# Two broadcasts on the way to TensorE: tiled products of 64 stationary columns in place of widened copies and full turns

## What is computed

```python
qb = apply_rope_2(rms_norm(heads(gq, GQA_Q_HEADS), q_gain[l]), cos, sin)     # 8 query heads of 64
kb = apply_rope_2(rms_norm(heads(gk, GQA_KV_HEADS), k_gain[l]), cos, sin)    # 2 key heads of 64
...
def softmax_attn(q, k, v):
    s = jnp.einsum('bgrqd,bgkd->bgrqk', q, k).astype(jnp.float32) * SCALE
    p = jax.nn.softmax(s, axis=-1).astype(v.dtype)
    return jnp.einsum('bgrqk,bgkd->bgrqd', p, v)
```

## Time and profile before

| what | value |
|---|---|
| median of 3 runs | 1810.4 us (1808.3 to 1814.79) |
| span of the profiled execution | 1814.2 us; the longest of the three runs, 1814.79 us, is 0.6 us above it |
| mean granted clock of TensorE | 0.995 |
| busy: PE, PEld | 1765.5 us (97%), 1444.1 us (80%) |
| busy: DVE, ACT, POOL | 930.4 us (51%), 899.4 us (50%), 1346.3 us (74%) |
| chain that ended last | PE 88%, DVE 6%, ACT 3% |

### The profile page before, as it was taken

How to read it: one execution, slowest core, us unless ns; L and a number is a source line. 1 busy time by engine, 2 the same in 40 slices (tenths; PEclk the granted TensorE clock), 3 DMA queues, 4 the chain that set the end, 5 groups by cost and what they waited for, 6 DMA issues and landing times.

```text
span 1814.2 us, 29552 instructions
## 1 busy us (share of the span) xinstructions
PE 1765.5 (97%) x10046; PEld 1444.1 (80%) x10046; DVE 930.4 (51%) x1898; ACT 899.4 (50%) x1404; POOL 1346.3 (74%) x776
## 2 busy tenths in 40 slices
PE   9988999979999999999999999999999999999997
PEld 7767888867888897788888977788888977788886
DVE  4567665563554554455555564545456665441112
ACT  6455444566444555644445455554446445554343
POOL 7368998434988687588888874588886894678884
PEclk9999999999999999999999999999999999999999
DMA  7767786424887644357886462368774563346552
GB/s 273 193 205 243 240 270 212 143 88 156 286 264 241 212 147 156 127 181 223 261 257 225 154 185 86 113 206 269 253 248 159 170 208 99 117 151 196 186 186 69
DMA packets 268425, 347.27 MB, mean 191 GB/s; under 512 B 20264, under 2 KB 181416, under 8 KB 268328
## 3 DMA queue, kind: packets, MB, share of 16 engines
q1 hardware_dynamic: 265152, 339.40, 58.6%
q10 hardware_dynamic: 3176, 6.62, 1.2%
HBM read 342.20 MB, written 1.64 MB: 190 GB/s over the span
## 4 chain that ended last, share of the span: by engine, by line
PE 88%; DVE 6%; ACT 3%; issue 1%; DMA 1%; POOL 0%; SPq 0%; ACTq 0%; DVEq 0%; POOLq 0%
PE bank L2447 23%; PE bank L2449 23%; PE bank L2448 23%; PE bank L2586 3%; PE bank L3187 2%; PE bank L2515 1%; PE bank L2517 1%; PE bank L2516 1%; PE bank L3177 1%; PE bank L3226 1%; PE bank L2610 1%; PE bank L2570 0%; DVE X L1547 0%; ACT wh L844 0%; ACT xf L928 0%
## 5 line engine op out<-in xcount | busy, mean ns | idle before, releaser
L807 POOL TENSOR_TENSOR wl<-raw,wh 128x1024 fp32r<-128x1024 f32 x300 | 730.7, 2445 | 112.1 <-ACT wh L1009 86.9
L2447 PE MATMUL bank<-wh,xh 128*128 128x512 f32 (+1 forms) x1590 | 625.2, 393 | 9.2 <-POOL wl L795 2.5
L2449 PE MATMUL bank<-wl,xh 128*128 128x512 f32 (+1 forms) x1590 | 612.4, 385 | 0.0
L2448 PE MATMUL bank<-wh,xl 128*128 128x512 f32 (+1 forms) x1590 | 611.2, 384 | 0.0
L794 POOL TENSOR_TENSOR wl<-raw,wh 128x512 fp32r<-128x512 f32 (+1 forms) x232 | 310.0, 1336 | 323.1 <-ACT wh L844 312.6
L1009 ACT ACTIVATE wh<-raw 128x1024 fp32r<-128x1024 f32 x270 | 286.5, 1062 | 434.9 <-PE bank L2449 424.7
L2447 PEld LDWEIGHTS bank<-wh,xh 128*128 128x128 f32 x1590 | 299.6, 188 | 71.7 <-issue 5.6
L844 ACT ACTIVATE wh<-raw 128x1024 fp32r<-128x1024 f32 (+2 forms) x268 | 275.0, 1049 | 155.7 <-PE bank L2449 88.3
L2449 PEld LDWEIGHTS bank<-wl,xh 128*128 128x128 f32 x1590 | 299.3, 188 | 61.0
L2448 PEld LDWEIGHTS bank<-wh,xl 128*128 128x128 f32 x1590 | 300.0, 189 | 55.2
L795 POOL TENSOR_TENSOR wl<-raw,wh 128x512 fp32r<-128x512 f32 (+1 forms) x232 | 309.9, 1336 | 0.0
(11 more groups left out here) (414 smaller groups left out, 2030.0 us busy)
## 6 DMA issues: line engine op xcount, KB each, us to landing
raw<-in_w_ffn_in SPq DMA_DIRECT2D x264, 256.0 KB, 3.0
raw<-in_w_in SPq DMA_DIRECT2D x224, 256.0 KB, 3.0
arena<-in_w_mod SPq DMA_DIRECT2D x76, 512.0 KB, 5.2
raw<-in_w_ffn_out SPq DMA_DIRECT2D x132, 256.0 KB, 3.5
raw<-in_l_w_gate SPq DMA_DIRECT2D x88, 256.0 KB, 3.8
raw<-in_l_w_up SPq DMA_DIRECT2D x88, 256.0 KB, 4.5
raw<-in_l_w_down SPq DMA_DIRECT2D x88, 256.0 KB, 4.1
raw<-in_w_o SPq DMA_DIRECT2D x48, 256.0 KB, 2.9
```

Of the source, the lines that this page charges most:

```text
L807: nc.gpsimd.tensor_tensor(wl[:, s, :], raw[:, s, :], words(wh)[:, s, :], ALU.subtract)\
L2447: mm(dst, x_hi, w_hi, start=first, stop=False, skip_group_check=True)
L2448: mm(dst, x_lo, w_hi, start=False, stop=False, skip_group_check=True)
L2449: return mm(dst, x_hi, w_lo, start=False, stop=last, skip_group_check=True)
```

## The change

The reciprocals are no longer copied 64 times: the stationary operand of a product reads the one column `rinv2[:, u]` 64 times over, and two such products (e = 0 and 1, at partitions 0 and 64 of bank 6) with the identity as moving operand take the place of one transpose. The keys are no longer copied twice: each head's 64 columns are the stationary operand of two products, at partitions 0 and 64. The tile `xf` is not used for either any more. With the copies, a `yield` of `head_norm` goes too.

```diff
@@ head_norm (DVE) @@
                         step(v.tensor_tensor(x2, x2, tb, ALU.add))
                         settle()
-                    for g in range(GKV):
-                        step(v.tensor_copy(kdup[:, t, P * g:P * g + P].rearrange("p (two d) -> p two d", two=2),
-                                           spread(x[:, nq + g:nq + g + 1, :], 2, HD)))
-                    if t == 0:
-                        yield
                 settle()
                 v.engine_nop().then_inc(qkv_ready, 1)
@@ sums (DVE) @@
-                    step(v.reciprocal(rinv2[:, at:at + 4], rsum2[:, at:at + 4]))
-                    settle()
-                    v.tensor_copy(rspread[:, c % 2, :].rearrange("p (u d) -> p u d", d=HD),
-                                  spread(rinv2[:, at:at + 4].unsqueeze(2), 4, HD)).then_inc(at_rinv, 1)
+                    v.reciprocal(rinv2[:, at:at + 4], rsum2[:, at:at + 4]).then_inc(at_rinv, 1)
@@ qk_turn (PE) @@
-                    turn(qk_banks(name, s)[b][1], src, qt_tr)
+                    to = qk_banks(name, s)[b][1]
+                    if what == "gq":
+                        turn(to, lambda i, t: gst[:, t, (2 * half + i) * P:(2 * half + i + 1) * P], qt_tr)
+                        return
+                    keys = gst_c1 if name == "c1" else gst
+                    for i in range(GKV):
+                        for t in range(TT):
+                            for e in range(2):
+                                at = GQH * HD + HD * i
+                                ins = mm(to[64 * e:64 * e + 64, SEQ * i + P * t:SEQ * i + P * t + P], keys[:, t, at:at + HD], ident,
+                                         start=True, stop=True, skip_group_check=True)
+                    ins.then_inc(qt_tr, 1)
@@ values (PE) @@
                     for qb in range(2):
-                        tr(bank[6][:, SEQ + qb * P:SEQ + qb * P + P], rspread[:, c % 2, qb * P:qb * P + P], ident)
+                        for e in range(2):
+                            u = 4 * (c % 2) + 2 * qb + e
+                            mm(bank[6][64 * e:64 * e + 64, SEQ + qb * P:SEQ + qb * P + P], rinv2[:, u:u + 1].broadcast_to([P, HD]), ident,
+                               start=True, stop=True, skip_group_check=True)
```

More of the change, by code:

```diff
@@ L448, in build @@
         v_windows = view("b2", len(WINDOWS), 512)
-        kdup, rspread = xf[:, :, 0:2 * P], xf[:, :, 2 * P:]
         m2 = view("b2", TT, D, at=bias_at)
@@ L3105, in qk_turn @@
                     pe.wait_ge(qkv_ready, ("c0", "x0", "c1", "x1").index(name) + 1)
-                    def src(i, t):
-                        f = slice((2 * half + i) * P, (2 * half + i + 1) * P)
-                        return {"gq": gst[:, t, 0:512], "gk": kdup[:, t, :]}[what][:, f]
                     if qt_at[name] or b:
                         pe.wait_ge(qt_ev, qt_at[name] + b)
-                    turn(qk_banks(name, s)[b][1], src, qt_tr)
+                    to = qk_banks(name, s)[b][1]
[10 more added lines that the diff above has]
+                    ins.then_inc(qt_tr, 1)
                 if name == "c1":
```

## The result

The changed kernel takes 1818.07 us (median of 20 runs, 1815.18 to 1834.65); the kernel before took 1813.49 us (20 runs, the three known before among them, 1807.53 to 1819.27). The ratio is 1.0032, with a 95% interval of 1.0017 to 1.0046: slower by about 5.8 us (3.1 to 8.3). It is not the quotient of the two medians, which lie 4.6 us apart; the same holds for the ratios of the experiments. The result is outside the predicted range, and the kernel became slower where the sum had it faster. Of the 9.1 us between the predicted 1809.0 and the measured 1818.07, 3.1 are not the change's: the median of the kernel before is 1813.49 over the 20 runs, and was 1810.4 over the three that the prediction had.

The account below looks back on a forecast made before the run. PE's own list was taken to bound the kernel, with about 2 us of waits within reach. Forms -0.15, waits -1.6 and -0.8, new wait +1.1 gave -1.45 us: 1809.0 from the median 1810.4, range 1804.5 to 1814.0.

Parts of the forecast that it names:

- A transpose is replaced by a plain f32 product: On PE, a plain product of 128 columns takes 0.11 to 0.12 us against 0.11 for a transpose: no extra cost.
- The price of a pair of 128 columns: Two products on 64-column tiles streaming the same identity: taken as 0.11 us, bounds 0.11 and 0.22.
- the pairs don't overlap: Rival: a pair's two products are served one after another, 7.0 us on top, +5.6 us, 1816.0; chance 0.05.
- a quarter of the transpose's rate: Rival: plain products take 0.44 instead of 0.11 us a pair, 21 us on top, 1830; chance 0.02.
- passes of the products (48 + 16 pairs): Reciprocals' 48 and keys' 16 product pairs on PE cost no more than the transposes they replace.
- changes of form: PE's switches of tile form: no difference for reciprocals, -0.15 us over the four key turns, `c1` gaining +0.30.
- wait of pair 2 gone: In `x0` and `x1`, PE's wait behind the key copies goes: 2 x 0.78 = 1.6 us gained.
- wait of the tile copy gone: Step 2 of `x0` and `x1`: the tile copy ends earlier, its 0.4 us wait goes twice, 0.8 us gained.
- new wait for pair 1: In `x0` and `x1`, multiplications moved ahead of step 4's maxima delay the reciprocal: 0 to 2.3 us, middle 1.1 taken.
- DVE 30 us less busy: Sign of being right: DVE's busy time falls by 30 us, from the 16 + 24 copies removed.

Follow-up runs that it names:

- e1: Kernel before, copies kept, with the 48 reciprocal and 16 key transposes written as full-array plain f32 products with the identity: 1821.96 us, ratio 1.0026.
- e3: Kernel before with all 288 transposes of the exponentials written as plain f32 products on the full array, reciprocals and keys untouched: 1847.31 us, ratio 1.0194.
- e4: Changed kernel with the reciprocals copied and transposed as before, so the keys' part stands alone: 1817.45 us, ratio 1.0002 against the kernel before.
- e5: Kernel before with the reciprocals' part of the change alone; keys' copies, their transposes and the `yield` kept: 1818.24 us, ratio 1.0005.
- e6: Kernel before, all copies and transposes kept, with odd steps' reciprocals made ahead of the row maxima and `output`: 1811.82 us, ratio 0.9990.

## Why the prediction was wrong

**The step that failed** is the price of a product, in the paragraph "A transpose is replaced by a plain f32 product" and in "The price of a pair of 128 columns". The value taken was 0.11 us for a pair of 128 columns; it is 0.22. The argument went by rows of the trace whose counts are passes and not products. The 24 records of the earlier trace rows are 12 products in the program: line 2850 runs over four heads, with one key tile for the first 128 queries and two for the second. The eight value products of the earlier trace rows are four: PE's list of the changed kernel, shown with the change, has value products x4 and x8 at lines 3195 and 3201, where the timeline above has x8 and x16. Taken by products, those rows give 0.24 us a product on the full array, and 0.44 us for two products of 256 columns on two tiles; a pair of 128 columns is half of that, 0.22. Both counts, the program's and the trace's, could be read before the result, and were not put beside each other. So what was taken for the kind of product costing nothing was one pass of it set against a whole transpose.

**The rival "the pairs don't overlap"** has the right size, 7.0 us, by the wrong mechanism. The pairs do overlap: eight records in 0.49 us are four pairs of 0.11 and 0.05, and e1 shows a loss of that size with no pairs at all. **The rival "a quarter of the transpose's rate"** has the right mechanism, and a factor of four where the runs show two (e1: 0.22 us more for two products at the place of the earlier trace rows, 0.11 each on the 0.11 of a transpose; e3: 0.12). The page TensorE: Matmul & The Clock Gate of the Trainium skill, section Terms, which the prediction set aside as not agreeing with the trace, was right in its direction; its figure is not what these runs measure.

**The other terms**, against what the starts show:

| term | forecast, us | measured, us |
|---|---|---|
| passes of the products (48 + 16 pairs) | 0 | +7.0 (64 times 0.11) |
| changes of form | -0.15 | -0.15 (`c1`: +0.77 less 0.44 is +0.33) |
| wait of pair 2 gone | -1.6 | -1.6 |
| wait of the tile copy gone | -0.8 | -1.3 |
| new wait for pair 1 | +1.1 | +2.3 |
| sum | -1.45 | +6.3, and +6.1 in the stretches |

- *Changes of form* held: the reciprocals' first start is 0.32 us behind the product, as forecast, and `c0` and `c1` come out at +1.98 and +0.77 for 2.05 and 0.74.
- *Pair 2* held: the wait is gone in both places, and both of its halves are seen apart in e4 and e5.
- *The tile copy* went as argued, but the term took the booked 0.4 us where that of pair 2 went by starts. By starts, turn to product is 1.28 us before and 0.63 in e6, which has no wait there: 0.65 us a place. 0.78 and 0.65 are the 1.43 us that e6 shows.
- *Pair 1* came at the upper of its two bounds, 1.15 us a place; it measured 1.16. The middle had been taken because a start 0.5 us apart decides; in the changed kernel both places fell on the same side, in e4 on different ones. SBUF — State Buffer of the Trainium skill, section Who interferes with whom, has an instruction of VectorE with two SBUF inputs contend with a GpSimd instruction that reads SBUF. The rows agree: 1.49 and 1.58 us beside a POOL instruction, 0.49 without one.
- *DVE 30 us less busy* can't be read off the page: 930.4 to 914.3 is 16.1, but DVE's busy time ahead of 640 us, which the change doesn't touch, rose by 8.0 (one instruction of the first block alone, line 1765 before and 1764 after, lasts 14.8 us here and 3.6 before). From 640 us on it fell by 24.2, from 555.41 to 531.25. The copies' 29.6 are gone, and about 5.3 came back in the rotation: of the three multiplications that moved ahead, the first two average 1.23 and 1.03 us where they averaged 0.58 and 0.75, the third stays at 0.49, and the rotation's last addition (line 2228) averages 0.87 for 0.49.
- *Slips without weight:* by the prediction's own terms the range is 1804.9 to 1814.4, and the sum passes 5.4 us from 63 pairs; the few hundredths said to go to either side went to "faster" alone.

With the price of a product right, the same sum would have read -1.45 and 7.0, or +5.6, close to the measured 6.1. That is partly luck: the waits' errors, +1.2 and -0.5, leave 0.7 us.

Left open: the 0.96 us by which the first score came later in this profiled execution than in that of before. It lies in work that the change doesn't touch, and other executions here were early by 2.7 us.

## What to carry to other kernels

Before a row's duration is used as the price of an instruction, put its count beside the count in the program; where they differ, the row prices a pass. An f32 transpose written as a product with the identity costs twice on TensorE, so a broadcast moved there from an engine with slack pays only where the waits it removes are worth more than the second pass (here 2.9 us against 7.0), and a new order of the slack engine's list may have the waits for nothing (e6, by the trace). When copies go from a list, what stood behind them moves ahead of something: follow that to the next result that another engine waits for.

## What the runs showed of the hardware

- A plain f32 product of 128 columns takes 0.22 us in two passes, a transpose 0.11 in one, at a granted clock of 1.00; on full and on 64-column tiles alike (e1, the changed kernel; in e3 the difference is 0.12 us).
- The time of a pass goes with the columns streamed: in `values(2)` of `x0` of the changed kernel, from pair to pair of records, 0.06 us for 64 columns, 0.11 for 128 and 0.22 for 256. A plain f32 product of 128 columns takes as long as one of the large `fp32r` products with 512 (0.23 us). No run here turned data with `fp32r` operands.
- Two 64-column tiles that stream the same identity run fully beside each other: eight passes in 0.49 us, two by two less than 0.01 us apart, the first 0.05 of it exposed.
- While POOL is busy, DVE's instructions with two SBUF inputs end one for one with POOL's, so whether one, two or three of the same three multiplications take 1.5 us instead of 0.5 changes from place to place and from kernel to kernel, and a wait of PE with it: 0, 1.1 or 1.9 us (e4, the changed kernel). That POOL is the cause is read from the times in the trace; no run took POOL away.
